# Delta rule of a decoder trunk: the first two inverse levels on 64x64 diagonal tiles, small blocks in two queues, the last late gate block between the pair products

## The reference: two layers of three token mixers and a channel mixer

```python
def step(state, inp):
    r_t, w_t, k_t, v_t, a_t, b_t = inp
    sa = jnp.einsum('bhij,bhj->bhi', state, a_t)
    state = (state * w_t[:, :, None, :] + sa[..., :, None] * b_t[:, :, None, :]
             + v_t[..., :, None] * k_t[:, :, None, :])
    y_t = jnp.einsum('bhij,bhj->bhi', state, r_t)
```

## Time and profile before

| what | value |
|---|---|
| median of 3 runs (least to most) | 2939.38 us (2938.31 to 2939.40) |
| the profiled execution | 2942.32 us, span 2940.5 us |
| mean granted TensorE clock | 0.982 |
| busy share of the span: PE, DVE, ACT, POOL | 95%, 76%, 40%, 20% |
| chain that ended last, by engine | PE 80%, DVE 12%, DMA 3%, ACT 3% |

### The profile page before, as it was taken

One profiled execution on the slowest core, in us unless ns is written; L12 is line 12 of the kernel. 1 busy time (PEld: TensorE's weight loads), 2 busy tenths in 40 slices (PEclk: granted clock), 3 DMA queues, 4 the chain that ended last, 5 costly groups with the idle time before them and its releaser, 6 DMA issues.

```text
span 2940.5 us, 49829 instructions
## 1 busy us (share of the span) xinstructions
PE 2798.0 (95%) x19146; PEld 2541.8 (86%) x19146; DVE 2246.3 (76%) x4294; ACT 1164.7 (40%) x1660; POOL 573.7 (20%) x354
## 2 busy tenths in 40 slices
PE   6999998998999999999999999889989999999998
PEld 6998887788999998877899987778989999977776
DVE  7999665669976658888789977655899666588887
ACT  4534321233444444333355342222444444433334
POOL 0000003111777630000000000020217777000000
PEclk9999999999999999999999999999999999999999
DMA  7553443154887778788745424241558777788875
GB/s 286 187 186 122 164 152 96 63 215 166 239 245 199 198 222 288 279 285 285 253 148 186 164 110 195 90 151 61 206 176 263 217 200 199 238 296 283 285 281 198
DMA packets 258979, 593.71 MB, mean 202 GB/s; under 512 B 82608, under 2 KB 198064, under 8 KB 200240
## 3 DMA queue, kind: packets, MB, share of 16 engines
q1 hardware_dynamic: 205456, 573.53, 55.8%
q0 software_dynamic: 36864, 0.15, 2.5%
q10 hardware_dynamic: 16416, 16.78, 1.7%
HBM read 537.27 MB, written 53.08 MB: 201 GB/s over the span
## 4 chain that ended last, share of the span: by engine, by line
PE 80%; DVE 12%; DMA 3%; ACT 3%; issue 2%; POOL 0%; SPq 0%; DVEq 0%; ACTq 0%; POOLq 0%
PE ps L1086 24%; PE ps L1065 18%; PE ps L666 12%; PE ps L628 6%; PE ps L689 3%; DVE u_lo L1929 2%; PE ps L1075 2%; PE ps L1015 2%; PE ps L756 2%; DMA act_rows<-region 2%; PE ps L706 1%; DMA ring<-in_stream 1%; DVE region L1570 1%; PE ps L943 1%; PE ps L956 1%
## 5 line engine op out<-in xcount | busy, mean ns | idle before, releaser
L1065 PE MATMUL ps<-h_hi,u_hi 128*128 128x256 f32 x2048 | 591.0, 289 | 32.0 <-DVE u_lo L1929 32.0
L1065 PE MATMUL ps<-h_lo,u_hi 128*128 128x256 f32 x2048 | 582.8, 285 | 0.0
L1065 PE MATMUL ps<-h_hi,u_lo 128*128 128x256 f32 x2048 | 582.8, 285 | 0.0
L2173 POOL DMA_INDIRECT gate_rows<-route x256 | 472.2, 1844 | 290.2 <-DVE route L2045 123.3
L1929 DVE TENSOR_TENSOR u_lo<-ring,u_hi 128x1024 fp32r<-128x1024 f32 x256 | 312.8, 1222 | 227.6 <-ACT u_hi L1362 201.1
L1065 PEld LDWEIGHTS ps<-h_hi,u_hi 128*128 128x128 f32 x2048 | 396.4, 194 | 34.7 <-DVE u_lo L1929 34.4
L1065 PEld LDWEIGHTS ps<-h_lo,u_hi 128*128 128x128 f32 x2048 | 396.8, 194 | 0.0
L1065 PEld LDWEIGHTS ps<-h_hi,u_lo 128*128 128x128 f32 x2048 | 396.1, 193 | 0.0
L1383 ACT ACTIVATE u_hi<-ring 128x1024 fp32r<-128x1024 f32 x192 | 203.9, 1062 | 323.5 <-PE ps L1086 323.5
L1936 DVE TENSOR_TENSOR u_lo<-ring,u_hi 128x1024 fp32r<-128x1024 f32 x192 | 234.8, 1223 | 51.4 <-ACT u_hi L1383 51.3
L1362 ACT ACTIVATE u_hi<-ring 128x1024 fp32r<-128x1024 f32 x256 | 269.5, 1053 | 0.0
(11 more groups left out here) (374 smaller groups left out, 5278.1 us busy)
## 6 DMA issues: line engine op xcount, KB each, us to landing
ring<-in_stream SPq DMA_DIRECT2D x456, 1024.0 KB, 7.6
act_rows<-region SPq DMA_DIRECT2D x256, 128.0 KB
gate_rows<-rstd ACTq DMA_DIRECT2D x2, 8192.0 KB, 26.2
region<-gate_rows SPq DMA_DIRECT2D x256, 64.0 KB, 3.9
region<-act_rows SPq DMA_DIRECT2D x128, 128.0 KB, 4.3
small_inverse<-act_rows SPq DMA_DIRECT2D x128, 128.0 KB, 4.1
gate_rows<-route POOLq DMA_INDIRECT x256
region<-in_c SPq DMA_DIRECT2D x7, 512.0 KB, 5.6
```

Source lines behind the costliest of these rows:

```text
L1065: ins = mm(ps[:, c % 4, 0:T], x, y[:, k, :], start=k == 0 and i == 0, stop=k == KD - 1 and i == 2)
L2173: gp.indirect_dma_start(gate_cells, bass.IndirectOffsetOnAxis(ap=gate_at[:, r:r + 1].bitcast(I32), axis=0), gate_weight[:, r:r + 1], None, ...
```

## The change, and its diff

1. The first two levels use 64x64 tiles. `XY` now holds, for each matrix, Y and X as 128 partitions by 64 columns: the upper left block in the upper 64 partitions, the lower right one in the lower 64. For each matrix PE multiplies the two `corners` one after the other, each in its own quarter of the array (rows and columns 0 to 63, or 64 to 127); both write their own partitions of the same columns of one bank. `Z1` has 64 columns in place of 128. In the second level only the upper Y is formed. Its X goes to a full tile `Xall`, whose lower left block is zeroed once and whose upper right block the third level fills by a copy where it added before. `u` reads `Xall`.
2. With 64 columns in place of 128, `block_mask` has four columns, and an expansion writes 2x64 elements.
3. POOL's expansions for the next group wait for the third level's updates (`dxy_mm`), not for `u_mm`.
4. PE waits for the group's masks ahead of the first level's updates, no longer ahead of Z1.
5. Of the DMAs for the diagonal blocks, SP issues four and ACT four, in both halves; for the small inverses the same in the first half; in the second SP issues all eight.
6. The last gate block is multiplied between the second and the third of four steps of pair products, into bank 7; ACT takes its sigmoid after its small-block loads; POOL waits for the block before it writes `Ct`.
7. DVE masks four of group 0's pair products ahead of the expansion, and the other four behind it.

In the diff, the code of SP, PE, ACT, DVE and POOL follows in that order behind the definitions.

```diff
-                  ("block_mask", 8), ("causal", 256), ("iota", 128), ("scan_keep", 256)):
+                  ("block_mask", 4), ("causal", 256), ("iota", 128), ("scan_keep", 256)):
...
-        XY = view(18944, GRP, 2, P)
-        Z1 = view(31232, GRP, P)
+        XY, Xall = view(18944, GRP, 2, HN), view(19968, GRP, P)
+        Z1 = view(31232, GRP, HN)
...
+            return ps[:, 7 if n == OUT - 1 else bank(n), :].rearrange("p (a t) -> p a t", a=2)
...
+        def store_diag(eng, i, b):
+            rows = slice(SUB * b, SUB * b + SUB)
+            eng.dma_start(diag_dram[i, b].rearrange("q r c -> r q c"), pre[i][rows, :, rows]).then_inc(diag_out[i], 16)
+
+        def load_small(eng, i, b):
+            rows = slice(SUB * b, SUB * b + SUB)
+            eng.dma_start(Wl[rows], small_dram[i, b].rearrange("q a r c -> r q a c")).then_inc(small_in, 16)
...
+                    for b in range(0, P // SUB, 2):
+                        store_diag(sp, i, b)
...
+                    for b in range(0, P // SUB, 1 if i else 2):
+                        load_small(sp, i, b)
...
-                project(LATE_GATE + 3, hT)
                 pe.wait_ge(S["tok_T_copied"], 8)
                 was_read(pe, LATE_GATE + 2)
-                was_read(pe, LATE_GATE + 3)
...
+                corners = slice(0, HN), slice(HN, P)
                 for s in range(0, GRP, 2):
+                    if s == 4:
+                        project(OUT - 1, hT)
                     pairs(0, s, True, True)
                 for g in range(4):
-                    pe.wait_ge(S["pairs_masked"], (g + 1) * GRP)
...
-                                if lev < LEVELS - 1:
-                                    ins = mm(ps[:, 4 + half, s * P:(s + 1) * P], Ct[:, q, :], XY[:, q, 0, :], start=True, stop=True)
+                                for rows in corners if lev < LEVELS - 1 else ():
+                                    ins = mm(ps[rows, 4 + half, cols], Ct[rows, q, rows], XY[rows, q, 0, :], start=True, stop=True)
...
+                            elif half == 0:
+                                pe.wait_ge(S["pairs_masked"], (g + 1) * GRP)
...
-                                    mm(ps[:, o, c0:c0 + P], XY[:, q, 1, :], Z1[:, q, :], start=True, stop=True)
-                                    ins = mm(ps[:, o, c0 + P:c0 + 2 * P], Z1[:, q, :], XY[:, q, 1, :], start=True, stop=True)
+                                for rows in corners[:2 - lev]:
+                                    mm(o[rows, 0:HN], XY[rows, q, 1, :], Z1[rows, q, :], start=True, stop=True)
+                                for rows in corners if lev < LEVELS - 1 else ():
+                                    ins = mm(o[rows, HN:], Z1[rows, q, :], XY[rows, q, 1, :], start=True, stop=True)
...
+                    if i % 4 == 3:
+                        act.wait_ge(S["pre_copied"], i + 1)
+                        for b in range(1, P // SUB, 2):
+                            store_diag(act, i // 4, b)
...
-                gate(LATE_GATE + 3)
+                act.wait_ge(small_out, 16)
+                for b in range(1, P // SUB, 2):
+                    load_small(act, 0, b)
+                act.wait_ge(used, taken(OUT - 1))
+                A(gate_tiles(OUT - 1), pair(OUT - 1), ACT.Sigmoid)
...
-                mask_pairs(0, *range(GRP))
+                mask_pairs(0, *range(GRP // 2))
+                vec.memset(Xall[HN:, :, 0:HN], 0.0)
                 ch.join(vec.memset(smid, 0.0))
                 dve.wait_ge(small_in, 16 * (P // SUB))
                 for half in range(2):
                     for j in range(4):
                         ins = vec.tensor_tensor(*expansion(0, half * 4 + j), ALU.mult)
                     ins.then_inc(S["expanded"], 1)
+                mask_pairs(0, *range(GRP // 2, GRP))
...
+                            if lev == 0:
                                 for a in range(2):
                                     vec.tensor_tensor(XY[:, hs, a, :], XY[:, hs, a, :], d[:, :, a, :], ALU.add).then_inc(S["dxy_added"], 1)
+                            elif lev == 1:
+                                vec.tensor_tensor(XY[0:HN, hs, 0, :], XY[0:HN, hs, 0, :], d[0:HN, :, 0, :], ALU.add).then_inc(S["dxy_added"], 1)
+                                for rows in (slice(0, HN), slice(HN, P)):
+                                    ins = vec.tensor_tensor(Xall[rows, hs, rows], XY[rows, hs, 1, :], d[rows, :, 1, :], ALU.add)
+                                ins.then_inc(S["dxy_added"], 1)
                             else:
+                                vec.tensor_copy(Xall[0:HN, hs, HN:], ps[0:HN, half * 2, 0:4 * HN].rearrange("p (s q) -> p s q", s=4)).then_inc(S["dxy_added"], 1)
...
-                    pool.wait_ge(S["u_mm"], 2 * g - 1 + half)
+                    pool.wait_ge(S["dxy_mm"], (g * LEVELS - 1) * 2 + half + 1)
...
+                pool.wait_ge(used, taken(OUT - 1))
```

More of the change, by code:

```diff
@@ L525, in _ @@
                     sp.wait_ge(S["pre_copied"], 4 * i + 4)
-                    for b in range(P // SUB):
-                        rows = slice(SUB * b, SUB * b + SUB)
-                        sp.dma_start(diag_dram[i, b].rearrange("q r c -> r q c"), pre[i][rows, :, rows]).then_inc(diag_out[i], 16)
+                    for b in range(0, P // SUB, 2):
+                        store_diag(sp, i, b)
                     sp.wait_ge(diag_out[i], 16 * (P // SUB))
@@ L536, in _ @@
                         sp.wait_ge(S["expanded"], 4)
-                    for b in range(P // SUB):
-                        rows = slice(SUB * b, SUB * b + SUB)
-                        sp.dma_start(Wl[rows], small_dram[i, b].rearrange("q a r c -> r q a c")).then_inc(small_in, 16)
+                    for b in range(0, P // SUB, 1 if i else 2):
+                        load_small(sp, i, b)
                 for n in range(RELAY, OUT + N_O):
@@ L618, in project @@
                 arrived(n)
-                bank_wait(pe, n)
+                if n != OUT - 1:
+                    bank_wait(pe, n)
                 w, o = blk[n % SLOTS], pair(n)
```

38 lines of the change are left out of this document (14 added, 24 removed).

## The result

The changed kernel takes 2923.24 us (median of 5 runs, 2919.1 to 2927.55), the kernel before 2939.4 us in the same session (2938.31 to 2945.48). The ratio is 0.9947, with an interval of 0.9934 to 0.996. That is 16.2 us saved where 31.4 were forecast. The forecast of 2908.0 was 15.2 us too low: the time lies outside the forecast's own range (2898 to 2917) and within the wide one, near its slow end.

The account below looks back on a forecast made before the run. The prediction took PE (80% of the chain) as the bound. Gains of 19.2 us a layer less 3.5 for the clock, 31.4 over both layers, gave 2908.0 us against 2939.4; own range 2898 to 2917, 8-in-10 range 2896 to 2925.

Parts of the forecast that it names:

- I take 0.9, 3.5 us a layer: Loss to low-clock stretches in the inverse stage: 0.9 us a group within bounds of 0 and 2, 3.5 a layer.
- the chain at full clock: The four groups' gains in the inverse stage without clock loss: 7.7 + 4.7 + 3.9 + 2.9 = 19.2 us a layer.
- Corner products at 0.030: First two levels: 64x64 products in diagonal quarters overlap within one bank, 0.030 us an instruction, 5.3 us a group.
- rival (a): First two levels: the quarters don't overlap, 0.057 us an instruction, gain 8.3 us a layer, 2922.8 us; chance 0.10.
- Groups at full clock: Gains worked out for each group of eight heads: first 7.7 us, second 4.7, third 3.9, fourth 2.9.
- DVE decides the third and fourth group: In the last two groups DVE's chain sets the time, so they gain 3.9 and 2.9 us.
- The second queue: First group's small-block loads: with one queue the last masks would wait up to 1 us, the second queue's worth.
- POOL's expansions and the stores on ACT at nothing: POOL's expansions lie beneath PE: 0; ACT's DMA issues at the first blocks' store: 0, between 0.5 us lost and gained.
- (b): Quarters overlap, but the clock is low through most of the levels and slows what follows: 2928.8 us; chance 0.13.
- (c): Levels with corners one behind the other and a low clock: 0.112 us an instruction, 16 us a layer slower, 2971; chance 0.06.
- (d): The stage ends earlier, but the weight blocks behind it don't come earlier, so nothing is left: 2937 us; chance 0.05.

Follow-up runs that it names:

- e9: The changed kernel with unused constant multiplications in PE's waits inside the levels, and two ring loads issued only after the third group's outputs: 2908.19 us, ratio 0.9893.
- e13: The changed kernel measured and profiled again, with nothing altered: 2924.1 us, ratio 0.9945.
- e1: The changed kernel with unused constant multiplications where PE waits inside the levels, loads left as they were: 2914.78 us, ratio 0.9923.
- e2: The changed kernel with each half's 64x64 products reordered, all of one corner and then all of the other: 2946.04 us, ratio 1.0033.
- e5: The changed kernel with DVE's group norm scaling in the third and fourth groups moved behind the third level's last copies: 2923.62 us, ratio 0.9939.
- e6: The changed kernel with all small-block DMAs issued by SP, in one queue: 2921.8 us, ratio 0.9941.

## Why the prediction was wrong

**The step that failed is "I take 0.9, 3.5 us a layer" for the clock.** The mechanism was named and its bounds (0 to 2 us a group, so up to 8 a layer) held it, but the value came from counting stretches instead of asking how much of the chain lies in them. Six stretches with 27.3 us a stage cost 151.8 - 145.03 = 6.8 us a layer, a quarter of their length (with all of it on PE's path it would be half). e9 shows that this is the clock and not a lesser overlap: with the gaps filled and the loads moved, the same instructions take what was worked out. e13 shows it with nothing added, at a third of the length (4.4 of 13.6 us). e1 alone does not, since its stop in the second group took back what the clock gave.

The 15.2 us by terms: clock 13.5 for 7.0, that is 6.5; the chain at full clock 36.4 for 38.4, 2.0; outside the stages 3.8; and 2.9 by which before's profile stood over its median and the changed kernel's did not. The last two are scatter as far as is known. By the means of four profiles each, the stages save 21.7 us and the span 17.7, so the clock's share of the miss is if anything larger (152.6 in place of 151.8 a stage).

**Corner products at 0.030: right.** Their instructions follow at 0.029 us (32 of them from 447.16 to 448.1), in two row tiles of one bank. The Trainium skill says in "TensorEngine Tiling (Array Packing)", section "Gotcha 1: PSUM Pressure", that row tiles can't use one bank at the same time; by this case's rows they do, when each writes its own partitions, and the price by that rule would have been rival (a)'s 0.057. e2 shows that value, and only when both neighbours use one quarter.

**Groups at full clock** (e9, second layer, against the profile of before): the first gains 7.4 us (0.5 at the last mask and 7.0 behind it; 7.75 worked out), the second 4.5 (4.7), the third 3.6 (3.9), the fourth 2.65 (2.9). Each is within 0.4 us. The third has the added multiplications in it: in e13's second layer, at full clock and without them, it takes 11.6 us from its last mask to its right-hand sides, against 12.4 in e9 and 14.45 before, and that gain is 2.9.

**DVE decides the third and fourth group:** right at full clock, where these sums hold; wrong as the changed kernel runs. e5 took DVE's part away and nothing came, since PE at 0.50 is as late. No run takes it away at full clock. A chain worked out at one clock doesn't tell who is next at the other.

**The second queue: up to 1 us.** e6 shows 0.9 in one layer and 0 in the other; too little for the median. The right size came by another way: the queue alone would be worth 0.1, the rest is the expansion that POOL holds up. The prediction didn't see that in the kernel before either, where the first expansion takes 1.14 us and the other seven 0.41; the new order gains these 0.7 us as well. In the changed kernel the expansions end at 440.64, and the masks wait for PE until 442.94.

**POOL's expansions and the stores on ACT at nothing:** no wait of PE in the stage names either, and the third gate block starts 7.93 us into the stage in both kernels.

**Rivals.** (a) fell by the rate, though its time, 2922.8, is what was measured: the right number for another reason. (b) is the nearest in kind: the clock is low in part of the levels and behind them, 27.3 us of 151.8, not through most. (c) fell, and e2 shows it for one order of the same instructions. (d) fell: in e9 the stages save 35.9 us and the span 34.5 (31.3 by the medians).

## What to carry to other kernels

Small tiles pay in full only at full clock, and a busy PE is no surety for it: e2 had PE busy for 17.08 of 17.10 us at 0.50. Price the half clock as a share of the chain, not by the number of stretches, and test the full-speed sum with a few multiplications of constants in the gaps. Then look whether the stage itself got shorter: e1 gained 7 us in the median and hardly one in its stages. Interleave the quarters in program order. Before you explain a remaining difference, cut unchanged code into stretches and compare several profiles of each kernel: here one stretch took 3.7 us more with the same work in four profiles against four, and other variants showed that it goes with neither kernel. When one row merges eight instructions, ask for the longest.

## What the runs showed of the hardware that was not expected

- The same 64x64 products take 0.029 us each in alternating corners and 0.107 in serial order, a factor of 3.7, nearly two of it from the overlap and two from the clock, which e2 lost for 54.6 us a stage although PE was busy 17.08 of 17.10 us there.
- Added multiplications and later loads together make the kernel faster: 2908.19 us against 2923.24, with stages of 145.50 and 145.03 us against 151.79.
- PE stood still for 2.02 us inside a run of products without a wait, under two ring loads, and didn't when they came later. In both layers one packet of the DMA queue that carries instructions (0.02 MB) lies in the gap, beside some fifty packets of the queue that the ring's loads use; in e9 such a packet comes alone near the same place and PE goes on. That PE was waiting for instructions fits this and is not shown.
- DVE's eight expansions take 1.71 us or, when they meet POOL's multiplication for `Ct` (e6, first layer), 2.60: one of them takes 1.18 us in place of 0.29. That the two engines get in each other's way in memory is a guess that fits all profiles.
